# The order of the steps of VectorE, ScalarE and GpSimd in the first two units of each SwiGLU of a hybrid decoder layer, and parameter copies moved to ScalarE

## The reference

```python
x = layer_norm(ALPHA * x + 0.5 * swiglu(x, ffn1_wg, ffn1_wu, ffn1_wd), ln1_g, ln1_b)
z = x @ w_in                       # six parts: C, B, h, p, g_a, g_p
y_a = B * conv3_causal(C * h)      # gated short convolution
y_p = pool_scale * blockdiag(mean_trailing_w(p) - p)      # w = 2, 4, 8, 16
x = layer_norm(ALPHA * x + (sigmoid(g_a) * y_a + sigmoid(g_p) * y_p) @ w_out, ln2_g, ln2_b)
x = layer_norm(ALPHA * x + 0.5 * swiglu(x, ffn2_wg, ffn2_wu, ffn2_wd), ln3_g, ln3_b)
# swiglu(x, wg, wu, wd) = (silu(x @ wg) * (x @ wu)) @ wd
```

## Time and profile before

| | us |
|---|---|
| median of 3 runs | 1045.77 |
| lowest, highest | 1044.98, 1049.0 |
| the profiled execution, its own time | 1046.54 |
| its span from first to last instruction | 1044.7 |
| TensorE busy in it | 1031.5 |
| VectorE busy in it | 711.8 |
| ScalarE busy in it | 482.5 |
| GpSimd busy in it | 460.4 |

### The profile page before, as it was taken

How to read it: one execution, slowest core, us unless ns; L and a number is a source line. 1 busy time by engine, 2 the same in 40 slices (tenths; PEclk the granted TensorE clock), 3 DMA queues, 4 the chain that set the end, 5 groups by cost and what they waited for, 6 DMA issues and landing times.

```text
span 1044.7 us, 21275 instructions
## 1 busy us (share of the span) xinstructions
PE 1031.5 (99%) x8592; PEld 1026.5 (98%) x8592; DVE 711.8 (68%) x1144; ACT 482.5 (46%) x735; POOL 460.4 (44%) x358
## 2 busy tenths in 40 slices
PE   8999999999999999999999999999999999999997
PEld 7999999999999999999999999999999999999997
DVE  6987977898755845822524325789888788977276
ACT  3665535645554452332332324456653565456335
POOL 4333444344348354844553546332425433443530
PEclk9999999999999999999999999999999999999999
DMA  8133343334327210532342334203333332432502
GB/s 256 52 102 102 102 121 87 103 97 122 112 83 195 82 40 13 156 103 85 87 117 67 113 89 127 67 14 102 91 112 102 102 116 77 132 101 82 144 20 82
DMA packets 195829, 103.32 MB, mean 99 GB/s; under 512 B 5188, under 2 KB 194260, under 8 KB 195725
## 3 DMA queue, kind: packets, MB, share of 16 engines
q1 hardware_dynamic: 195651, 101.86, 33.9%
q10 hardware_dynamic: 82, 0.12, 0.1%
HBM read 99.74 MB, written 2.48 MB: 98 GB/s over the span
## 4 chain that ended last, share of the span: by engine, by line
PE 93%; DVE 3%; issue 1%; DMA 1%; ACT 0%; SPq 0%; POOL 0%; DVEq 0%; ACTq 0%; POOLq 0%
PE ps L1641 19%; PE ps L1642 19%; PE ps L1643 19%; PE ps L1664 10%; PE ps L1661 10%; PE ps L1662 10%; PE ps L1710 2%; PE ps L1717 1%; PE ps L1711 1%; PE ps L1785 1%; DMA xrow<-in_x_prompt_dram 1%; PE ps L1764 1%; PE ps L2123 0%; DVE xl L1087 0%; DMA raw<-in_ffn_wg_dram 0%
## 5 line engine op out<-in xcount | busy, mean ns | idle before, releaser
L672 POOL TENSOR_TENSOR wl<-raw,wh 128x512 fp32r<-128x512 f32 (+1 forms) x168 | 223.9, 1362 | 328.7 <-DVE raw L1147 313.0
L719 ACT ACTIVATE wh<-raw 128x1024 fp32r<-128x1024 f32 (+4 forms) x183 | 210.4, 1154 | 175.0 <-DMA raw<-in_ffn_wg_dram 57.8
L1642 PE MATMUL ps<-form_lo,wh 128*128 128x260 f32 x640 | 181.5, 284 | 0.0
L1643 PE MATMUL ps<-form_hi,wl 128*128 128x260 f32 x640 | 181.3, 283 | 0.0
L1641 PE MATMUL ps<-form_hi,wh 128*128 128x260 f32 x640 | 181.3, 283 | 0.0
L1661 PE MATMUL ps<-xh,wh 128*128 128x260 f32 x640 | 166.9, 282 | 0.0
L1662 PE MATMUL ps<-xl,wh 128*128 128x260 f32 x640 | 166.5, 282 | 0.0
L1641 PE MATMUL ps<-xh,wh 128*128 128x260 f32 x536 | 152.1, 284 | 2.8 <-POOL wl L672 2.1
L1642 PE MATMUL ps<-xl,wh 128*128 128x260 f32 x536 | 151.8, 283 | 0.0
L1643 PE MATMUL ps<-xh,wl 128*128 128x260 f32 x536 | 151.5, 283 | 0.0
L659 POOL TENSOR_TENSOR wl<-raw,wh 128x512 fp32r<-128x512 f32 x63 | 88.0, 1396 | 138.9 <-ACT wh L719 138.8
(11 more groups left out here) (288 smaller groups left out, 2478.5 us busy)
## 6 DMA issues: line engine op xcount, KB each, us to landing
raw<-in_ffn_wg_dram SPq DMA_DIRECT2D x80, 256.0 KB, 3.3
raw<-in_w_in_dram SPq DMA_DIRECT2D x40, 512.0 KB, 4.0
b<-in_ffn_wu_dram SPq DMA_DIRECT2D x40, 256.0 KB, 3.4
raw<-in_ffn_wu_dram SPq DMA_DIRECT2D x40, 256.0 KB, 3.0
raw<-in_ffn_wd_dram SPq DMA_DIRECT2D x16, 512.0 KB, 5.5
raw<-in_ffn_wd_dram SPq DMA_DIRECT2D x24, 256.0 KB, 3.5
raw<-in_ffn_wd_dram SPq DMA_DIRECT2D x24, 192.0 KB, 2.9
raw<-in_w_out_dram SPq DMA_DIRECT2D x7, 512.0 KB, 3.8
```

The source lines that it names most:

```text
L672: nc.gpsimd.tensor_tensor(slots(wl_slot, s, p), slots(raw_slot, s, p), slots(wh_slot, s, p).bitcast(F32), ALU.subtract).then_inc(lo_ready, 1)
L719: return nc.scalar.activation(out, in_, ACT.Copy)
L1642: mm(out, hi, vl, start=False, stop=False, skip_group_check=more)
L1643: ins = mm(out, lo, vh, start=False, stop=n == count, skip_group_check=more)
```

## The change

On VectorE: `parameters()` is gone, ScalarE does the same three copies right after its first rounding of a form. In the second SwiGLU the weight sums of unit 2 stand ahead of a wait for the normalised activations. `last_sum` of unit 2 stands ahead of `hid_opened`. Unit 1 takes its results (`gate_first`, `up_first`, and now `up_second(1)` too) ahead of the sums and rests of tile 1, and `rest_thirteen` of unit 2 stands behind `up_first(1)`. Unit 2 has a list of its own, `second_unit`, that begins with `hid_pair(1)` and ends with `mid_rests(1)`. On ScalarE `round_twenty_four` of unit 2 stands ahead of `hid_up(1, 3)`, and `round_mid(1)` moves to unit 2. On GpSimd the B11 part of unit 3 waits for `t13_made` instead of `t4_made`.

```diff
@@ split_unit, GpSimd
-                pool.wait_ge(t4_made, unit_no(n, p))
+                if p == 3:
+                    pool.wait_ge(t13_made, unit_no(n, p))
+                else:
+                    pool.wait_ge(t4_made, unit_no(n, p))
                 for name in ("B11", "B21", "B22"):
+                    if name == "B21":
+                        pool.wait_ge(t4_made, unit_no(n, p))
@@ ScalarE
+            def parameters():
+                act.wait_ge(cols_made, K + 2)
+                copy(par[:], ps[:, 7, 0:10 * K]).then_inc(cols_read, 1)
+                copy(conv_state[:].rearrange("p k b s -> p (k b s)"),
+                     ps[:, 7, 128:128 + K * NS * CS]).then_inc(cols_read, 1)
+                copy(pool_state[:].rearrange("p g b s -> p (g b s)"), ps[:, 6, 0:G * NS * PS]).then_inc(cols_read, 1)
@@ unit_steps, ScalarE
                     keep(first_u, x_bank, "P6", u_taken)
                     if p == 1:
                         hid_up(0, 1)
-                        hid_up(1, 3)
                     if p < NU:
                         round_twenty_four(n, p + 1)
-                    if was[0] != "down":
+                    if p == 1:
+                        hid_up(1, 3)
+                    elif p == 2:
+                        round_mid(1)
+                    if p > 1 and was[0] != "down":
                         round_mid(was[1])
@@ ffn_steps, ScalarE
                 round_form(n, 0)
                 if n == 0:
+                    parameters()
                     round_thirteen(n, 1)
@@ VectorE
-            def parameters():
-                dve.wait_ge(cols_made, K + 2)
-                read.on(copy(par[:], ps[:, 7, 0:10 * K]))
-                read.on(copy(conv_state[:].rearrange("p k b s -> p (k b s)"), ps[:, 7, 128:128 + K * NS * CS]))
-                read.on(copy(pool_state[:].rearrange("p g b s -> p (g b s)"), ps[:, 6, 0:G * NS * PS]))
@@ up_steps, VectorE
                 def first_unit():
-                    t_two(n, 2)
-                    rest_thirteen(n, 2)
-                    last_sum(n, 2)
-                    for f in range(2):
-                        mid_sums(f, (1, 3)[f])
-                        hid_rest(f, (1, 3)[f])
+                    hid_opened(0)
+                    hid_opened(1)
+                    mid_sums(0, 1)
+                    hid_rest(0, 1)
+
+                    dve.wait_ge(s.hid_made, 2)
                     gate_first(1)
                     up_first(1)
+                    rest_thirteen(n, 2)
+                    up_second(1)
                     rest_twenty_four(n, 2)
+                    mid_sums(1, 3)
+                    hid_rest(1, 3)
+
+                def second_unit():
+                    hid_pair(1)
+                    weight_sums(n, 3)
+                    t_two(n, 3)
+                    hid_rest(2, 0)
+                    mid_sums(2, 0)
+                    last_sum(n, 3)
+                    rest_thirteen(n, 3)
+                    gate_first(2)
+                    up_first(2)
+                    rest_twenty_four(n, 3)
+                    mid_rests(1)
@@ unit_steps, VectorE
                     if p == 1:
                         first_unit()
+                    elif p == 2:
+                        second_unit()
@@ up_steps, VectorE
                 if n == 1:
+                    weight_sums(n, 2)
+                    t_two(n, 2)
                     dve.wait_ge(norm[1].biased, 8)
                 form_sums(n)
                 if n == 0:
-                    parameters()
                     weight_sums(n, 1)
                     t_two(n, 1)
                     last_sum(n, 1)
@@
-                weight_sums(n, 2)
+                if n == 0:
+                    weight_sums(n, 2)
+                    t_two(n, 2)
                 form_rest(n, 2)
                 form_rest(n, 3)
-                hid_opened(0)
-                hid_opened(1)
+                last_sum(n, 2)
```

## The result

| | before | changed |
|---|---|---|
| median of 9 runs, us | 1045.95 | 1050.37 |
| lowest, highest, us | 1044.98, 1049.71 | 1046.69, 1053.72 |
| profiled execution, its own time, us | 1046.54 | 1046.69 |
| its span, mean granted clock | 1044.7, 0.993 | 1044.9, 0.995 |

The ratio is 1.0037, 95% interval 1.0022 to 1.0052: slower, by less than 0.5% at the median. The one profiled execution of the changed kernel is its fastest run, so its span of 1044.9 says little about the median.

The account below looks back on a forecast made before the run. TensorE, busy 1031.5 of 1044.7 us, was taken as the bound. 0.4 + 2.55 + 1.6 = +4.6 us on 1046.54 gave 1051.1, less 0.77 for the median 1050.4; own range 1049 to 1051.6, 8-in-10 range 1046.8 to 1052.8.

Parts of the forecast that it names:

- the 4.75: Units 1 and 2 of both SwiGLUs: the most the change can give, 2.22 + 1.64 + 0.89 us, 0.45% of the time.
- 1.64 us put down to the clock: First SwiGLU, P1 and Q5 of unit 2: 4.52 us instead of 2.88 at a granted clock of 0.50.
- 1.18 was laid out: First SwiGLU: `rest_thirteen(2)` is slowed beside GpSimd, so Q5 of unit 2, due at 48.75, starts at 49.93.
- The early P1: First SwiGLU: P1 of unit 2 starts on time at 47.31, and its 2.22 us stall is gone.
- 1.69 laid out: First SwiGLU, unit 2: VectorE stands still 1.69 us before `hid_rest(2, 0)`, waiting for ScalarE's rounding of tile 2.
- 13.2: From Q4 of unit 1 to Q4 of unit 2 VectorE needs 13.2 us, TensorE only 10.1.
- the 0.4 laid out at Q5 of unit 3: First SwiGLU: `rest_thirteen(3)` holds Q5 of unit 3 up by 0.4 us.
- +0.4 us in the first SwiGLU: Q4 of unit 2 starts at 64.55 instead of 64.14, using up the whole gain; -0.55 with the better port outcome.
- +2.55 in the second: Second SwiGLU: late `up_second(2)` lets TensorE go on at 731.6 instead of 729.0, +2.55 us.
- The early sums in the second opening: Second SwiGLU: `weight_sums(2)` and `t_two(2)` during the wait for the biases cost nothing, or up to 0.5 us.
- One of the two waits is followed by a fall: Gaps before Q4 of unit 2 in both SwiGLUs: one half-clock fall, 1.6 us, bounds 0 and 3.3; chance 0.35.
- +4.6: Whole kernel: sum of 0.4 + 2.55 + 1.6 us on the profiled 1046.54, giving 1051.1.

Follow-up runs that it names:

- experiment 4: Changed kernel with `up_second(2)` ahead of `rest_twenty_four(3)`, tile 2 and `first_u` ahead of `round_thirteen(3)`, GpSimd's unit 2 B21, B22 waiting for `t13_ready`: 1040.69 us, ratio 0.9957.
- the second profile of before: The kernel before, unaltered, profiled again; VectorE's second operation in the opening started behind GpSimd's third lo part: 1048.89 us.
- experiment 5: The kernel before with only the parameter copies moved from VectorE to ScalarE: 1045.93 us against 1045.82, ratio 0.9996.
- 7: Changed kernel with only GpSimd's B21 and B22 parts of unit 2 waiting for `t13_ready` of unit 2: 1050.1 us against 1045.82, ratio 1.0038.
- experiments 2: Changed kernel with ScalarE's rounding of tile 2 and copy of P6 (`first_u`) ahead of `round_thirteen(3)`: 1044.95 us against 1045.52, ratio 0.9996.
- 3: Changed kernel with `up_second(2)` ahead of `mid_rests(1)`, and tile 2 and `first_u` ahead of `round_thirteen(3)`: 1043.64 us against 1045.52, ratio 0.9981.
- 6: Changed kernel with unit 2's VectorE list back in the old order and `round_mid(1)` behind `second_gate(1)`: 1049.25 us against 1045.82, ratio 1.0033.
- Experiments 1: Changed kernel with `up_second(2)` moved ahead of `mid_rests(1)` at the end of unit 2's list: 1046.8 us against 1045.52, ratio 1.0018.
- the fourth profile: The changed kernel, unaltered, profiled a fourth time, with the slow opening: 1057.78 us, the slowest of all.
- the second set: The changed kernel, unaltered, run again beside the experiments, 10 runs: 1053.28 us against 1045.82 for the kernel before, ratio 1.0059.

## Why the prediction was right, point by point

**What bounds it, and the most there was to gain.** Right: the differences that repeat stand in TensorE's waits in units 1 to 3. Most of it can be had: to Q5(4) experiment 4 needs 4.3 us less than the first profile of before in the two SwiGLUs together. That its median gains 4.8, as the 4.75 laid out, is partly luck: the second profile of before has only 1.2 us to give in these places, and the mean clock of experiment 4's runs is 0.9961 beside 0.9934. The 4.75 was also split wrongly. Of the 1.64 us put down to the clock only 0.4 were its own: in experiment 5's profile, with the same late P1 of unit 2 and no fall, TensorE waits for `up_second(1)` instead, and Q4(2) comes at 25.09 instead of 25.49.

**Unit 1.** Right: P1 of unit 2 starts at 8.66 us after P1 of unit 1 instead of 10.89, and Q5 of unit 2 waits 1.35 us where 1.18 was laid out, because `rest_thirteen(2)` stands behind GpSimd's third operation. Experiments 4 and 7 show that it is GpSimd: 2.33 becomes 1.22 when GpSimd waits. The Trainium skill, page "SBUF — State Buffer", section "Who interferes with whom", says that the shared port pair is an exclusive lock and that issue order decides who blocks. The traces agree: 1.1 us are lost where GpSimd's operation of 1.29 us began 0.05 us sooner, and in the opening the time goes from 0.68 to 2.89 us with the order of the two starts. The early P1 is not as firm as I had it: in experiments 2, 3, 6 and 7 it waited 0.35 to 1.0 us for `hid_rest(0)`.

**Unit 2.** The two sizes that carry the forecast are right: 1.65 us of stand-still ahead of `hid_rest(2, 0)` (1.69 laid out), 1.2 us of `mid_rests(1)`, and 13.1 us from Q4 to Q4 (13.2). Experiments 1 and 2 take each of them away alone and 3 both, down to 10.14. What I missed is where TensorE waits. By the prediction's own times P7 of unit 2 would start at 57.14, four products after Q4 of unit 1; the copy of P6, which stands behind the two copies that end at 57.65, would end near 57.9. I did not hold the one against the other. So a wait of 0.84 us stands at P7, and the one at Q4 of unit 2 is 2.05 instead of 2.65; the 0.4 laid out at Q5 of unit 3 is not there. VectorE sets the end either way.

**The nets.** +0.4 us in the first SwiGLU became +0.60 to Q4(2) and +0.64 to Q5(4), with the fall of before counted in; against experiment 5's profile, which has none, it is 1.0. +2.55 in the second became +2.04 and +2.13: `round_unit(3)` started 11.3 us after P1 of unit 1, not the 11.9 of before, since its block landed sooner. That wait is real, though, and it varies: in the fourth profile the same rounding waited 2.38 us for its block and Q4(2) came at 26.18, and in the first SwiGLU of that profile it waited 1.91 us and Q4 to Q4 took 14.17. With `hid_pair(1)` at the head of the list all of VectorE hangs on this landing; in the kernel before `weight_sums(3)` and what follows went ahead. The early sums in the second opening cost nothing, as forecast: from Q5(4) to P1 of unit 1 of the second SwiGLU it takes 632.28 us, and 632.22 in experiment 5, neither with a fall. GpSimd's earlier B11 of unit 3 was not tried by itself.

**The clock.** "One of the two waits is followed by a fall" was a choice between bounds, from two waits of before; three of eight is what four profiles show, 1.5 us each in place of 1.64. On 19 runs the mean clock is 0.9935, beside 0.9934 and 0.9945 of before.

**The sum.** +4.6 was forecast; +4.4 and +7.5 were measured at the medians of two sets. By the pieces as measured (0.64, 2.13, and three falls in four profiles at 1.5 each, an estimate) it would be +3.9. The agreement to 0.1 us with the first median is luck: it goes by a choice of one fall, the second set lies 3 us higher, above the stated range, and one thing was left out. In executions with the slow opening there is nothing to gain in unit 1, and the loss in unit 2 stays. Between the two profiles with that opening the changed kernel is 3.83 us slower to Q5(4) in the first SwiGLU and 3.67 in the second, of which about 1.1 and 1.5 us are the late landings. How often the opening goes that way was not measured: of the thirteen profiles two had it. The spread of the changed kernel, 1046.7 to 1057.8, has these sources in the profiles: 0, 1 or 2 falls behind the new waits (1.5 each), a fall between the SwiGLUs (1.3), the opening (5.3 and 6.5), the landings, and 2 us at the end that have no known cause. How they share in the 3 us between the two medians stays open.

**The copies.** Right, and small: 0.85 us on ScalarE in a pause. That they shorten GpSimd's wait by as much was not seen in experiment 5.

## What to carry to other kernels

When a list of steps on one engine is put in the order of need, lay it beside the lists of the engines that it hands to and takes from: the loss here was a step on VectorE that wanted ScalarE's second piece of work while ScalarE's first waited for VectorE. Moving the next unit's release (`up_second`) ahead of one step that nobody waits for took 1.2 us off Q4 to Q4 in the second SwiGLU, beside 1.7 and 1.3 for ScalarE's order. And hold each result's time against every consumer of its bank, not only against the consumer of its value.

## What the runs showed that I had not expected

- In the opening the meeting of VectorE and GpSimd decides between two courses of the whole execution: two operations of VectorE with both inputs in SBUF take 1.86 or 3.90 us, depending on whether the second of them starts ahead of GpSimd's third part or 0.04 to 0.14 us behind it, and with the half clock behind it unit 1 starts at 37 to 39 or at 44.
- It is the order that counts and not how early GpSimd is: in the changed kernel's first profile its third part starts sooner than in either slow case, at 19.08 instead of 19.39, but VectorE's second operation is sooner still (17.28), and the opening is the short one.
- The same wait of 1.9 us was followed by half clock in three cases of eight, so a single profile can be 3 us longer or shorter by two falls alone; the starts of products in the first SwiGLU, counted from the unit's first, repeat to 0.1 us where no fall, landing or slow opening shifts them.
